# A float32 encoder layer on one core: where the statistics array stands in memory, and the order of VectorE's and ScalarE's work for the first pair of feed-forward columns

## The reference

```python
def conv_ffn(hn, w_ffn_in, conv_w, conv_b, w_ffn_down):
    u, v = jnp.split(hn @ w_ffn_in, 2, axis=-1)      # hn: 768 x 1024, u and v: 768 x 2816
    up = jnp.pad(u, ((0, 0), (pad, pad), (0, 0)))
    uc = conv_b
    for t in range(CONV_W):                          # width 3, along the tokens
        uc = uc + up[:, t:t + L] * conv_w[t]
    return (jax.nn.gelu(uc) * v) @ w_ffn_down

h = h + token_mixer(rmsnorm(h, norm_mix), ...)
h = h + conv_ffn(rmsnorm(h, norm_ffn), ...)
y = rmsnorm(h, norm_final)
```

## Time and profile before

| | |
|---|---|
| median of 3 runs | 1280.01 us (1275.86, 1280.44, 1280.01) |
| profiled execution, its own time | 1277.07 us |
| its span, first to last instruction | 1275.3 us |
| PE busy | 1244.8 us, 98% of the span |
| DVE (VectorE), ACT (ScalarE), POOL busy | 711.9, 490.8, 129.1 us |
| instructions | 18036 |

### The profile page before, as it was taken

How to read it: one execution, slowest core, us unless ns; L and a number is a source line. 1 busy time by engine, 2 the same in 40 slices (tenths; PEclk the granted TensorE clock), 3 DMA queues, 4 the chain that set the end, 5 groups by cost and what they waited for, 6 DMA issues and landing times.

```text
span 1275.3 us, 18036 instructions
## 1 busy us (share of the span) xinstructions
PE 1244.8 (98%) x7088; PEld 1120.5 (88%) x7088; DVE 711.9 (56%) x969; ACT 490.8 (38%) x724; POOL 129.1 (10%) x93
## 2 busy tenths in 40 slices
PE   6999999999999999999999988999999999999998
PEld 5999899999999988888888878998789998789986
DVE  7494585486478362233223697775237774337755
ACT  5352353335145151222121355553125543135534
POOL 0000000000000000000000304330123320124200
PEclk9999999999999999999999998999999999999999
DMA  4311211101111112111114012122212113102122
GB/s 169 135 39 45 68 45 50 62 33 49 64 47 49 34 47 70 66 50 66 66 66 166 33 57 76 67 67 83 83 34 67 67 50 119 63 34 82 51 83 99
DMA packets 23180, 86.10 MB, mean 68 GB/s; under 512 B 2512, under 2 KB 2768, under 8 KB 23120
## 3 DMA queue, kind: packets, MB, share of 16 engines
q1 hardware_dynamic: 22544, 83.90, 19.1%
q10 hardware_dynamic: 576, 1.38, 0.3%
HBM read 82.12 MB, written 3.15 MB: 67 GB/s over the span
## 4 chain that ended last, share of the span: by engine, by line
PE 94%; DVE 4%; ACT 1%; DVEq 1%; issue 1%; DMA 0%; SPq 0%; ACTq 0%
PE ps L1417 58%; PE ps L1661 24%; PE ps L1514 3%; PE ps L1454 3%; PE ps L1507 1%; PE ps L1524 1%; PE ps L1442 1%; DVE af L1192 1%; PE ps L1444 1%; DVE h L1132 1%; DVE ring L1145 1%; PE ps L1399 0%; PE ps L1490 0%; PE ps L1499 0%; PE ps L1495 0%
## 5 line engine op out<-in xcount | busy, mean ns | idle before, releaser
L1417 PE MATMUL ps<-hn,ring 128*128 128x256 f32 (+1 forms) x2544 | 465.2, 338 | 0.3 <-DVE hn L834 0.3
L1417 PEld LDWEIGHTS ps<-hn,ring 128*128 128x128 f32 x2544 | 385.7, 189 | 51.6 <-issue 0.7
L1661 PE MATMUL ps<-af,ring 128*128 128x384 f32 x1848 | 328.2, 340 | 11.1 <-DVE v L1229 5.6
L1661 PEld LDWEIGHTS ps<-af,ring 128*128 128x128 f32 x1848 | 324.0, 189 | 15.1 <-issue 5.9
L1417 PE MATMUL ps<-ring,g 128*128 128x512 f32 x792 | 186.0, 395 | 0.8 <-issue 0.8
L1417 PEld LDWEIGHTS ps<-ring,g 128*128 128x128 f32 x792 | 148.4, 188 | 37.6 <-issue 2.0
L805 DVE TENSOR_TENSOR ring<-raw,ring 128x1024 fp32r<-128x1024 f32 x68 | 83.2, 1224 | 121.4 <-ACT ring L411 117.0
L460 ACT ACTIVATE sig<-ps 128x768 f32<-128x768 f32 x36 | 29.2, 811 | 182.2 <-PE ps L1417 182.2
L411 ACT ACTIVATE ring<-raw 128x1024 fp32r<-128x1024 f32 x68 | 71.6, 1055 | 29.7 <-PE ps L1417 11.1
L1145 DVE TENSOR_TENSOR ring<-raw,ring 128x512 fp32r<-128x512 f32 x88 | 73.6, 871 | 16.5 <-ACT ring L648 16.5
L1376 POOL TENSOR_TENSOR sums<-raw 128x512 f32<-128x512 f32 x1 | 1.3, 1292 | 711.3 <-DMA raw<-in_pairs 711.3
(11 more groups left out here) (158 smaller groups left out, 1220.9 us busy)
## 6 DMA issues: line engine op xcount, KB each, us to landing
raw<-in_units SPq DMA_DIRECT2D x90, 512.0 KB, 3.5
raw<-in_pairs SPq DMA_DIRECT2D x44, 512.0 KB, 3.5
strips<-in_strips SPq DMA_DIRECT2D x4, 896.0 KB, 4.5
x_in<-in_x_s SPq DMA_DIRECT2D x4, 512.0 KB, 5.4
h<-in_x_s SPq DMA_DIRECT2D x1, 2048.0 KB, 7.9
y_s<-hw SPq DMA_DIRECT2D x4, 512.0 KB, 2.6
x_in<-in_x_p SPq DMA_DIRECT2D x2, 512.0 KB, 7.4
h<-in_x_p SPq DMA_DIRECT2D x1, 1024.0 KB, 10.2
```

The source lines that it names most:

```text
L1417: ins = pe.matmul(out, w if stationary_w else x, x if stationary_w else w, start=start and i == 0, stop=stop and i == 2)
L1661: ins = pe.matmul(ps[:, bank, 0:HALF], ring[:, p, a, k * P:(k + 1) * P], af[:, x, b, k, :], start=first and k == 0 and j == 0, stop=k == H ...
```

## The change

`stat` is taken out of the persistent arrays and placed behind the end of every region, so that the regions begin where `stat` began. VectorE's order for pairs 0 and 1 is rewritten: the low parts of (1,A11) and (1,A12) come before the token forms of tile 4; of those forms S1 and S4 are made later, each beside the same form of tile 5; `join_third(0)` and `join_first(0)` change their places around `combine_second`; and `combine_second` makes S1, S2, S3 in place of S1, S3, S2, with S3 waiting for nothing. ScalarE's wait for pair 1's combined weights follows that order, and its `first_copy(1)` is moved ahead of the loop.

```diff
+REGION = 4 * (NT * D + 2 * 8 * T + 3072 + 4 * T + HALF + 14 * HK * HALF)
@@ memory
-        stat = persistent("stat", [P, 6, NT])
@@ behind the last region
+        _, stat = region(("f0", [P, REGION // 4], F32), ("stat", [P, 6, NT], F32))
@@ hi_piece, ScalarE
-                    act.wait_ge(t_done, 4 * i + (S1, S3, S2, A22).index(x) + 1)
+                    act.wait_ge(t_done, 4 * i + ((S1, S2, S3, A22) if i == 1 else (S1, S3, S2, A22)).index(x) + 1)
@@ ScalarE, ahead of the loop
             third_copy(0)
+            first_copy(1)
             for lo, hi in CHUNKS:
...
-                    if i > 0:
+                    if i > 1:
                         first_copy(i)
@@ combine_second, VectorE
                 elif x == S3:
-                    dve.wait_ge(t_done, 5)
                     ins = dve.tensor_tensor(b12, b22, b12, ALU.subtract)
@@ VectorE, ahead of the loop
-            for x in SUMS:
-                combine_tokens(dve, 1, x, s_done, 4)
             lo_upto(BASE + 3)
+            combine_tokens(dve, 1, S3, s_done, 4)
+            combine_tokens(dve, 1, S2, s_done, 4)
             weigh2(5)
             combine_tokens(dve, 2, S3, s_last, 0)
             combine_tokens(dve, 2, S2, s_last, 0)
             lo_upto(BASE + 4)
             lo_form(4, S2)
             lo_form(5, S2)
+            combine_tokens(dve, 1, S1, s_done, 4)
             combine_tokens(dve, 2, S1, s_last, 0)
...
             lo_form(5, S3)
+            combine_tokens(dve, 1, S4, s_done, 4)
             combine_tokens(dve, 2, S4, s_last, 0)
             lo_upto(BASE + 7)
             lo_form(4, A22)
             lo_form(5, A22)
-            join_first(0)
             lo_upto(BASE + 8)
             lo_form(4, S4)
             dve.wait_ge(flo, ORD[0, S2] + 1)
             lo_form(5, S4)
+            join_third(0)
             combine_second(S1)
+            combine_second(S2)
+            join_first(0)
             combine_second(S3)
-            combine_second(S2)
@@ VectorE, in the loop
                     lo_upto(PLACE[i, S3] + 5)
-                    join_third(i)
+                    if i > 0:
+                        join_third(i)
```

## The result

The change makes the kernel faster: the median of four runs is 1263.37 us (1262.84 to 1264.54) against 1279.94 for four of the kernel before, a ratio of 0.9879 with a 95% interval of 0.9857 to 0.9900. The two profiled executions stand closer to each other: 1264.54 and 1277.07 us, with spans of 1262.7 and 1275.3, so 12.6 us have to be found in the traces. One of the later runs of the kernel before, 1757.25 us at a mean granted clock of 0.658, is left out of every median and difference here.

The account below looks back on a forecast made before the run. PE was taken as the bound, busy 1244.8 of 1275.3 us. Memory was costed at nothing and the order at 3.0 less 0.6, so 1278.3 - 2.4 = 1275.9 us, range 1271.3 to 1280.7.

Parts of the forecast that it names:

- What bounds the kernel: Whole kernel: PE, busy 1244.8 of 1275.3 us; time can come only from matmul pace, PE's pauses and the low-clock stretch.
- Part one: Memory: `stat` moved, so regions and `ring` share remainder 128; forecast no gain, bounds 3.3 us gained or 3.6 lost.
- the fourth combination: PE's operands, moving and stationary both at remainder 128, the one combination absent from the trace; costed at nothing.
- Doesn't do what it says: Rival on memory: remainder 128 instead of 0 could void any effect of a true multiple of 512; falls together with forecast.
- the pace: Rival: new addresses settle PE at its lower pace everywhere, 2.1 + 1.2 us on top, 1272.6 us; chance 0.26.
- the addresses are all: Rival: misplaced operands cause all excess over half the low-clock duration; 79 us go, about 1197 us; chance 0.04.
- half of 512: Estimate for 256-column matmuls in the addresses are all: excess of 10 ns each, half of that of 512 columns.
- Part two: VectorE and ScalarE order in the first pairs: 3.0 us gained up to (1,S1), less 0.6 before (1,A22), 2.4 net.
- The half-clock rival: Clock falls again after the 3.1 us pause before (1,S1), deciding at about 3.5; 3.1 us lost, 1279.0 us; chance 0.19.
- The other side: Rival: with the new addresses all three chunks run at 176.5 ns, 3.6 us lost against 2.4 gained, 1279.5 us; chance 0.08.
- The sum's base: Whole kernel: mean of four runs of the kernel before, 1278.3 us, from which the forecast gain is taken.
- The widest rival: The rival the addresses are all: 79 us gained, about 1197 us; chance 0.04.

Follow-up runs that it names:

- e1: Only `stat` moved behind all regions, order of VectorE and ScalarE as in the kernel before; 1265.29 us, ratio 0.9901 to the kernel before.
- e5: Not the layer: only fp32r matmuls, 18 operand distances at 512, 384, 256 columns; 512 columns took 226.7 ns at distance 0, 234.3 at 160.
- e6: Matmul-only scan like e5 with both operands' remainders moved; 512 columns took 226.7 ns wherever both stood at the same multiple of 32.
- e4: As e1, with 32 unused bytes ahead of `raw`, so distances 0 and remainders 160; 1266.03 us, ratio 0.9909 to the kernel before.
- e2: The new order alone against the kernel before, `stat` left where it was; 1276.55 us, ratio 0.999.
- e12: The kernel before, unchanged, profiled once more; 1280.49 us, where another run of the same program beside it took 1277.39.
- e11: Matmul-only scan like e5, distances 0, 64, 160 six times each at different start moments; 512 columns took 226.7, 228.9, 234.3 ns, all six alike.
- e7: The changed kernel with `stat` back in front and 96 unused bytes behind it, distance 256; 1263.47 us, ratio 0.9890 to the kernel before.
- e9: The changed kernel with `hn` and `gated` 64 bytes further and `merged` 256; 1262.15 us, ratio 0.9875 to the kernel before.
- e8: The changed kernel with `join_last(0)` moved earlier in VectorE's order, to the end of pair 0's turn; 1262.06 us, ratio 0.9876 to the kernel before.
- e10: The changed kernel with the changes of e8 and e9 together; 1260.56 us, ratio 0.9868 to the kernel before.
- e3: As e1, with all regions 64 bytes further and `ring` left at remainder 128; 1269.32 us, ratio 0.9932 to the kernel before.

## Why the prediction was wrong

*What bounds the kernel* was right: all that changed the time changed PE's pace, pauses or clock.

*Part one failed, at the step "I cost the fourth combination at nothing".* It was worth 11.3 us in the two profiles (12.4 without the later rise of the clock at the start), and 12.6 in e1; the bounds given were 3.3 gained and 3.6 lost. The reading behind it took hn (288 moving, 128 stationary) and g (the reverse) as "one off" and qsplit, klow as "both off", found all three near 400 ns, and concluded that being off costs nothing. But the quantity that counts is the difference. hn was at 160 and g at -160, both in the slow class (234 and 233 in e5 and e6). Two rows that differed in what I had named were alike in what mattered. The third row was the only one at distance 0 and should have shown the fast pace. It went from 396 to 390 ns although its own distance did not change. The trace of before has the reason. Of these 32 matmuls, 28 are followed by one of hn, whose weights lie in `ring`, at a distance of 160: they take 396.4 ns, and the next starts 233.9 ns behind. The other 4 are followed by one of `kdup`, which lies in the regions too: 389.0 and 228.5 ns. So the fast row was there, in 4 matmuls, and the distance that counts looks to be that to the weights that are loaded next, while the operand moves; four matmuls suggest it, no run tried it by itself.

*"Doesn't do what it says"* rested on a true observation, remainders of 128 and not 0, but e4 shows that it is without effect. The part was better than its name: it makes both remainders equal.

*The rival "the pace"* had the direction and one term right, the second chunk: 2.1 us forecast, 2.1 by its pace and 1.8 by its starts. Its other term, hn at 1 ns each, was 4.9. It left g and `merged` out, 6.8 us together, because the trace of before gave no fast group for 512 columns.

*The rival "the addresses are all"* had the kind of cause right, the place of PE's operands in memory, and its price wrong: 79 us for 12. That PE's two reads meet there is argued from the distances, not seen. It took the whole excess over half of the low-clock duration as misplacement. At distance 0, 512 columns take 226.7 ns, so 6.6 of the 20 ns went, 384 columns stay at 173.3, and 256 columns became 1.4 ns slower, a sign that the estimate of "half of 512" excluded. The figure of 216 ns from the Trainium skill, "TensorE: Matmul & The Clock Gate", "Back-to-back issue gap", was not reached by any run here.

*Part two was right up to (1,S1).* Forecast were 1.2 to 2 us before (0,S4) by `join_first`, 3.1 before (1,S1) by `join_last`, none before (1,A11), and a gain of 3.0; the rows show 1.44, 2.88, none, and 3.0. The 0 to 0.6 us before (1,A22) were 0: `third_copy(1)` ended at 776.11, 1.4 us ahead of (1,A22) at 777.50. The half-clock rival, at 0.19, is what happened behind (1,S1), and so the net was 1.3 for 2.4. It came at a pause of 2.88 us, below the 3.5 at which I had put its point of decision, and lasted half as long as taken, so it cost 1.56 for 3.1. The 3.5 was the time from one last matmul to one fall; a fall behind a shorter pause was in none of the rows it was read from.

*The other side* (all chunks at the higher pace) did not come: no profile with distance 0 shows it. In e2 and e12, at the old distances, it came in the third chunk.

*The sum's base*, 1278.3 as a mean of four, was fair: the two sessions gave 1277.88 and 1277.57. The chance for faster by over 0.5% was 0.28, too low because no unknown of part one was allowed more than 3.6 us: both bounds came from a pace that the trace showed for 384 columns only, although a pace of 512 columns at another distance was nowhere in it. The widest rival had 0.04, and between it and the next, 3 and 79 us, nothing stood.

## What to carry to other kernels

Where PE bounds a float32 kernel (fp32r matmuls; no other type was run), write down for each group of matmuls the address of the moving operand less that of the stationary one, modulo 256 bytes, and keep it at 0 for 512 columns and off 0 for 256; unused bytes ahead of an array are enough, and both should stay at multiples of 32. Rows that seem to show that a placement is without effect must differ in the quantity that acts, so group them by every combination of the addresses, the difference first. When an engine's queue is reordered around one wait, look for the next one that the old pause covered (here 5.6 became 1.4 + 2.9, and that became 1.9), and price the clock behind it.

## What the runs showed of the hardware that was not expected

- PE's pace depends on where its two operands stand to each other. In fp32r, 512 columns take 226.7 ns at a distance of 0 or 256 bytes, 228.9 at 64, 233 to 234 at other multiples of 32, and up to 237.7 if the addresses are no multiples of 32. At multiples of 32, 384 columns take 173.3 to 176.7 and 256 columns 113.3 to 120.1, with 0 among the slowest (e5, e6). The Trainium skill, page "SBUF — State Buffer", section "Who interferes with whom", says that "PE and ACT never wait on anyone" and calls PE's two read ports independent. That PE waited for another engine's reads no run here shows; but in e5, with no other engine at work beside PE, the distance of PE's own two operands alone moved 512 columns from 226.7 to 234.3 ns, so as to each other the two reads are not without effect here. Which parts of the memory meet was not measured.
- The same program can run a chunk at 173.3 or at 176.5 ns per matmul at a distance of 160 bytes (e12), and 256 columns can run at 113.3 or 117.8 ns with the operands at the same two addresses (e6 against e5 and e11). What picks it is open: the start moments and PSUM banks of e11 didn't.
- The clock fell for 3.4 us behind the pauses of 2.88 to 2.91 us before (1,S1) in all four profiles that have one, 1.5 (after), 1.4 (e2), 0.5 (e7) and 0.4 us (e9) after matmuls had resumed. Behind pauses of 1.8 us it may or may not: it fell in e8 (1.87 us) and not in e10 (1.84), and in e4 behind the 1.80 before (1,A11), where before, e1, e3 and e12 with the same pause kept it. It is a term of 1.6 us that comes or stays away between executions.
- At the start, too: the same first 24 matmuls of 256 columns took 3.69 us in one execution of the kernel before and 4.77 in another.
